# Router logits on TensorE: tokens held still, or weights held still in four strips

## What is computed

```
u = rms_norm(x) ; projections ; mLSTM heads and differential-attention heads
h = x + concat(head outputs) @ w_out
u2 = rms_norm(h) * norm2_g
logits = u2 @ router_w + router_b        # 1024 tokens x 32 experts
top_vals, top_idx = top_k(logits, 4) ; gates = softmax(top_vals)
h = h + sum over the 4 experts of gate * expert(u2)   # clamped SwiGLU, 1024 wide
out = rms_norm(h)
```

## Time and profile before

| | us |
|---|---|
| runs, median of 3 | 2183.54 |
| runs, lowest and highest | 2183.42 and 2188.01 |
| profiled execution: span, first to last instruction | 2178.9 |
| profiled execution: route stage, products of tile 1 to the end of the loop | 502 to 603 |
| profiled execution: PE busy | 2127.2 (98%) |

### The profile page before, as it was taken

The page is one execution under the profiler, slowest core; times in us unless marked ns, Lnnn a source line. Parts: engine busy times, 40 slices in busy tenths (PEclk is TensorE's granted clock), DMA queues, the critical chain, the costliest instruction groups (busy, mean ns, idle before and its releaser), DMA issues. The chain is left out here.

```text
span 2178.9 us, 35969 instructions
## 1 busy us (share of the span) xinstructions
PE 2127.2 (98%) x11236; PEld 1808.1 (83%) x11237; DVE 1711.6 (79%) x2144; ACT 1374.5 (63%) x1753; POOL 413.9 (19%) x433
## 2 busy tenths in 40 slices
PE   7999999989979999999999999999999999999998
PEld 7987878768869998888888889988889998888884
DVE  5426767787688778879879878779987779988896
ACT  4324655553466656767767767568775657867675
POOL 0000000003331221312212212214221123221120
PEclk9999999999979999999999999999999999999996
DMA  4110101218867778979979969779997669998897
GB/s 164 45 49 35 58 34 46 102 57 228 230 242 287 253 251 293 369 248 385 363 249 384 373 238 353 242 257 380 386 371 250 246 239 353 379 359 321 303 376 276
DMA packets 106785, 548.76 MB, mean 252 GB/s; under 512 B 17989, under 2 KB 28742, under 8 KB 51818
## 3 DMA queue, kind: packets, MB, share of 16 engines
q1 hardware_dynamic: 88154, 504.91, 61.6%
q0 software_dynamic: 18576, 43.12, 8.2%
HBM read 516.46 MB, written 41.47 MB: 256 GB/s over the span
## 5 line engine op out<-in xcount | busy, mean ns | idle before, releaser
L2505 DVE TENSOR_TENSOR wl<-raw,wh 128x2048 fp32r<-128x2048 f32 x423 | 958.4, 2285 | 41.5 <-PE sums L2264 27.7
L2368 ACT ACTIVATE wh<-raw 128x2048 fp32r<-128x2048 f32 x425 | 804.9, 1912 | 123.0 <-DMA raw<-in_w_experts 41.8
L2248 PE MATMUL sums<-wh,xx 128*128 128x512 f32 x832 | 325.8, 392 | 0.0
L2247 PE MATMUL sums<-wl,xx 128*128 128x512 f32 x832 | 325.5, 391 | 0.0
L2246 PE MATMUL sums<-wh,xx 128*128 128x512 f32 x832 | 325.0, 391 | 0.0
L2180 POOL DMA_INDIRECT h_dram<-y,pairs_mine x47 | 125.1, 2662 | 758.9 <-DVE y L2601 413.9
L2246 PE MATMUL sums<-wh,al 128*128 128x512 f32 x560 | 226.8, 405 | 0.5 <-DVE al L2592 0.2
L2248 PE MATMUL sums<-wh,ah 128*128 128x512 f32 x560 | 219.0, 391 | 0.0
L2247 PE MATMUL sums<-wl,ah 128*128 128x512 f32 x560 | 218.2, 390 | 0.0
L2247 PEld LDWEIGHTS sums<-wl,xx 128*128 128x128 f32 x832 | 156.7, 188 | 34.0
L2248 PEld LDWEIGHTS sums<-wh,xx 128*128 128x128 f32 x832 | 156.7, 188 | 33.3
(11 more groups left out here) (420 smaller groups left out, 4180.3 us busy)
## 6 DMA issues: line engine op xcount, KB each, us to landing
raw<-in_w_experts SPq DMA_DIRECT2D x426, 1024.0 KB
raw<-in_w_chan SPq DMA_DIRECT2D x20, 512.0 KB, 3.2
o_gate<-in_x SPq DMA_DIRECT2D x8, 512.0 KB, 5.4
raw<-in_w_out SPq DMA_DIRECT2D x8, 512.0 KB, 4.3
ht<-in_x SPq DMA_DIRECT2D x8, 512.0 KB, 6.4
h_dram<-ht SPq DMA_DIRECT2D x8, 512.0 KB
u_dram<-ut SPq DMA_DIRECT2D x8, 512.0 KB
h_all<-h_dram SPq DMA_DIRECT2D x8, 512.0 KB, 7.6
```

Source lines behind the costliest of these rows:

```text
L2247: pe.matmul(out, hi[:, n, :], w_lo[:, kk, :], start=False, stop=False)
L2248: last = pe.matmul(out, hi[:, n, :], w_hi[:, kk, :], start=False, stop=half == 1 and kk == 3)
L2368: nc.scalar.activation(wh[ch % HIGHS][:, :, :], raw[ch % RAW][:, :, :], ACT.Copy).then_inc(h_split.sem, 1)
L2505: dve.tensor_tensor(wl[ch % LOWS][:, :, :], raw[ch % RAW][:, :, :], wh[ch % HIGHS][:, :, :], ALU.subtract).then_inc(l_split.sem, 1)
```

## The change

The eight logits matmuls of a tile change roles: the router's 32 columns of weights are now stationary and the 128 tokens of `uT` move. The output is experts on partitions, 32 of them, and feature tile n goes to the strip of partitions `n % 4`, so that four strips of the array's columns each add up two feature tiles in `l_ps[:, 128:256]`. DVE copies that 128x128 block to a new buffer `lp4` (`parts_out`), and one fp32 matmul with `lp4` stationary and `pick_cons` (four 32x32 identities on top of each other) moving adds the four strips and turns the result back to tokens on partitions, in `l_ps[:, 0:32]`, where the bias is added as before.

On PE the strips are placed ahead of the last two feature tiles (six matmuls) of the next tile's products, and the adding matmul behind them. `logits` and `top` count twice per tile. PE waits for `b_loaded` 112 before the first pair.

```diff
-    logits = S("logits", 2, credit=1)
-    top = S("logits_biased", 2, credit=1)
+    logits = S("logit_parts_then_logits", 4, credit=2)
+    top = S("logit_parts_out_then_biased", 4, credit=2)
...
+        lp = sb("lp4", [P, P])
...
-                    act.wait_ge(logits.sem, logits.at(i, p))
+                    act.wait_ge(logits.sem, logits.at(i, 2 * p - 1))
...
                     if more:
-                        for n in range(KT):
-                            last = products(q, 1, n)
-                        last.then_inc(o_made.sem, 1)
-                    pe.wait_ge(top.sem, top.at(i, p))
+                        for n in range(KT - 2):
+                            products(q, 1, n)
+                    pe.wait_ge(top.sem, top.at(i, 2 * p - 1))
...
-                        last = pe.matmul(l_ps[:, 0:E], uT[:, n, :], rw[:, n, :], start=(n == 0), stop=(n == KT - 1))
+                        strip = slice(n % 4 * E, n % 4 * E + E)
+                        last = pe.matmul(l_ps[strip, P:2 * P], rw[:, n, :], uT[:, n, :], start=n < 4, stop=n >= 4)
                     last.then_inc(logits.sem, 1)
+                    if more:
+                        for n in range(KT - 2, KT):
+                            last = products(q, 1, n)
+                        last.then_inc(o_made.sem, 1)
+                    pe.wait_ge(top.sem, top.at(i, 2 * p + 1))
+                    pe.matmul(l_ps[:, 0:E], lp[:, :], k.pick_cons[:, :], start=True, stop=True).then_inc(logits.sem, 1)
...
             pe.wait_ge(small_loaded.sem, small_loaded.at(0, 48))
+            pe.wait_ge(b_loaded.sem, b_loaded.at(0, 112))
...
+                parts_out(i, 1 - p)
                 dve.wait_ge(o_made.sem, o_made.at(i, p + 1))
...
+            def parts_out(i, p):
+
+                dve.wait_ge(logits.sem, logits.at(i, 2 * p + 1))
+                dve.tensor_copy(lp[:, :], l_ps[:, P:2 * P]).then_inc(top.sem, 1)
...
                     if not is_last(i):
+                        parts_out(i, p)
                         residual(i + p, 1 - p)
                     elif p == 0:
                         last_residual(i, 1)
+                    else:
+                        parts_out(i, p)
...
-                    dve.wait_ge(logits.sem, logits.at(i, p + 1))
+                    dve.wait_ge(logits.sem, logits.at(i, 2 * p + 2))
```

## The result

| | before | after |
|---|---|---|
| median, us (14 runs each, same chip) | 2181.64 | 2188.01 |
| lowest and highest, us | 2178.67, 2188.01 | 2185.16, 2190.33 |
| span of the profiled execution, us | 2178.9 | 2185.7 |

What follows compares the result with a forecast made beforehand. PE bounds the kernel, busy 98% of the span. Wait +3.2, clock +1.7, strips -4.7, stalls +2.3 and +0.1, tile 6 +0.8, end -0.3 and -1.0 give +2.1: 2185.5 us; own range 2182.5 to 2188.5, wider 2180.5 to 2191.5.

Steps and rivals of the forecast that it cites:

- The wait: Ahead of its first pair PE stands for the last table load, pick_cons: +3.2 us, bounds 2.9 and 3.4.
- The clock: Behind PE's table wait the granted clock may fall to 1.2 GHz over dense products: +1.7 us, bounds 0 and 3.4.
- Strips side by side: Logits on PE: four column strips overlap, so their block takes 0.79 us a tile; one after another 2.05.
- (a): Rival: strips don't run side by side, block 2.05 us, 0.48 lost a tile; +13.0, time 2196.5 us; chance 0.13.
- (b): Rival: strips run two at a time, block 1.20 us, 0.38 saved a tile; +5.3, time 2188.8 us; chance 0.10.
- The speed of 3.2 for four strips: Alternative estimate by the skill's rule: strip stream 1.71 / 3.2 = 0.54 us, block 0.88, forecast half a microsecond later.
- The saving: Per tile on PE, logits go from 1.80 to 1.01 us: 0.79 saved, six blocks -4.7; residual to residual 13.2.
- DVE's copy: DVE's 128x128 copy of the parts from PSUM, 0.29 us, covered by six products on PE: costs nothing.
- New stalls: Strips wait for copied transposes, +2.3 us (bounds 1.0 and 3.7), and transposes for the normed tile, +0.1.
- Tile 6 and the end: Tile 6's strips come before the last residual, +0.8 us; its biased logits gain 0.3, the last tile's logits 1.0.
- Rival (c): The table wait hides, so 3.2 and 1.7 go: sum -2.8, time 2180.7 us; chance 0.12.

Runs made afterwards that it cites:

- the filled wait: Changed kernel plus fourteen 512-column products that nothing uses, on PE ahead of its b_loaded wait: 2180.89 us (before 2180.85), ratio 1.0000.
- the kernel with the early table: Changed kernel with pick_cons loaded right behind router_b and PE's wait for b_loaded removed: 2178.86 us (before 2180.85), ratio 0.9988.

## Why the prediction came out as it did

- **The wait.** Forecast 3.2 us, first product at about 505.3. It started at 506.20 in a trace whose first residual was 1.0 us later. From the residual's start to the product's are 2.82 us; before it started 0.26 us ahead of it (502.09): 3.1 us. Right, and shown by the two kernels that have it alone or lack it.
- **The clock.** Forecast 1.7, bounds 0 and 3.4. This is the term that failed in size, and twice. The stretch behind the wait came in its full length of 6.83 us and cost 2.9 us (after against the filled wait); the 1.7 was a mean between none and all of it, and both kernels with this wait unfilled had all of it. And there was a second stretch, 549.88 to 553.29, that no sentence foresaw: tile 2 took 15.75 us and tile 3 14.03, with the filled wait 15.08 and 13.22: 1.5 us. Together 4.4 instead of 1.7, outside the bound of 3.4. Why the second came in after and not in the filled kernel, whose strips waited as long, no run shows.
- **Strips side by side**, rivals (a) and (b). Forecast a block of 0.79 us a tile. From the last product ahead to the third one behind (604.12 to 605.59, single instructions of after's trace) are 1.47 us, less three starts of 0.227: 0.79. The serial and the paired block, 2.05 and 1.20 in the rivals, were measured by the same distances as 2.07 and 1.21. The rule that weight loads overlap only between row groups, in the Trainium skill ("TensorE: Matmul & The Clock Gate", "Part 3: Packing small matmuls"), does not hold for these strips: all have the same 128 rows, and sixteen passes with their sixteen loads take 0.57 us up to the next product. The prediction's own rows spoke against it already: in the earlier trace rows a load of 128 rows starts at 583.69, 0.01 us behind the start of a product on the same 128 rows. The speed of 3.2 for four strips, which the prediction had estimated from the same section of the Trainium skill, is near what the whole block shows from the first strip to the next product, 1.87 / 0.57 = 3.3, its fill included; the prediction had applied it to the moving columns alone, and those run four times as fast.
- **The saving.** Forecast 0.79 us a tile, and residual to residual 13.2. Measured were 13.20 and 13.24 in tile 5, which has no stall (after and filled wait), but before took 13.90 in that tile and not the rounded 14.0, so that 0.70 and 0.66 were saved. PE's starts in after's tile 5 show where the rest lies: rank and transposes take 1.23 us and not 1.19, and the four products behind the strips start 0.236 us apart in place of 0.227, another 0.04. These two terms were put at nothing. What makes them longer no run shows.
- **DVE's copy** at nothing: right; PE waits for it in the last tile alone (0.69 us).
- **New stalls.** Forecast 2.4; tile 1 0.61 (0.7), tile 2 1.69 (1.4 to 1.9), and 1.15 in tile 4, where 0.2 for four tiles had been taken. The bound of 3.7 held them. The step left out a transfer: in tile 4 ACT's copy stands behind DVE's work on mix rows, which land with nothing to spare, and the row of that wait in before (0.8 us) was not read.
- **Tile 6 and the end.** Forecast +0.8, then -0.3 - 1.0. From R6 to the last half of the last residual are 13.22 us, 14.01 before (606.72 and 598.12 at its end): the block in tile 6, as taken. From there to the last biased logits are 8.87 us, 10.25 before: -1.38, forecast -1.3. They come 2.45 us behind the last tile's first strip, forecast 2.4. Right; but behind it PE's wait for the experts' first rows was 3.2 us and not 2.7, and the prediction had not looked for this wait.
- **Rival (c)**, the wait hides: its premise is false here, but its number was good for the kernel in which the wait is really gone: 2.8 us under before, measured 2.0.

The account over R0 to R6, in which 90.13 us stand against 81.76: wait 3.1, clock 4.4, stalls 3.45, and -3.1 for six strip blocks and five products with the identities in place of five old blocks (4.7 + 1.1 - 9.0): +7.8 of +8.4. The other 0.6 us is, but for 0.1, that the five tiles behind the first saved 0.70 us each and not 0.79, and that the first paid a little more. Another -0.8 and -1.4 follow up to the last logits, -0.5 behind them, and +1.0 lay ahead of R0, which came anywhere from 501.7 to 504.4 in these traces and is no part of the change. By the sum of the prediction, +2.1 against +6.8 by the two spans, the clock was 2.7 us too low, the stalls 1.0 and the saving 0.5 too high; R0's +1.0 and the -0.5 behind the logits, both within what traces differ by, are most of the rest.

## What to carry to other kernels

A change to an inner step may add a dependence at the stage's entry; here one line of waiting cost more than three times what eight faster tiles gained. Price such a wait together with the clock that may fall behind it, as separate outcomes rather than as a mean (here low stretches of 0, 3.41 and 6.83 us were seen), fill it with work where it can't be removed, and load a small table ahead of large ones that are needed later. When tiles get shorter, read which transfer lands with the least to spare, since it takes the gain first. Set the time of the profiled execution beside the median of the runs before a wait in its trace is made the next target.

## What the runs showed beyond what was expected

- The moving columns of fp32 column strips overlap fully. One, two and four 32-column strips with 128 moving columns: sixteen passes to the next product in 1.87, 0.99 and 0.57 us.
- A product of two passes with a stationary operand of 32 or 64 rows, between products of 128 rows, has 0.36 us of idle time ahead of its load and costs 0.30 us more than one of 128 rows.
- What stood ahead of a low clock in the tiles, from seven kernels: PE waits of 2.92, 3.55 and 3.88 us each went with 6.83 us at 1.2 GHz, which began in the wait; one of 2.30 was followed by 3.41 us, one of 2.55 by none. Of four waits of 1.65 to 1.69 us one was followed by 3.41 us, three by none. So over these lengths the wait alone does not decide, and what else does stays open. The stretch behind the 3.88 us, from the kernel with the early table:

```profile
502.00:570.50 68.50, 63.37 (x361) 51.43 (x359) 49.17 (x151) 26.11 (x39) 23.50 (x18) 1.00 0.81 186
570.56:577.39 6.83, 5.20 (x27) 4.02 (x28) 3.12 (x6) 1.58 (x2) 3.92 (x4) 0.50 0.97 336
```
